# Layer norms of block one: sums taken behind the residual, statistics in two columns, each half normalised in the other half's feed-forward

## The reference

```python
for i in range(2):
    m_lat = jnp.split(cond_lat @ ada_w[i] + ada_b[i], 6, axis=-1)   # m_ctx in the same way
    a_lat = h_lat * (1 + m_lat[1]) + m_lat[0]
    a_ctx = h_ctx * (1 + m_ctx[1]) + m_ctx[0]
    y_ctx, y_lat = mixer(a_ctx, a_lat)             # layer 0: retention, layer 1: neighbourhood
    h_lat = layer_norm(ALPHA * h_lat + m_lat[2] * y_lat, ln_g[i, 0], ln_b[i, 0])
    f_lat = swiglu(h_lat * (1 + m_lat[4]) + m_lat[3], ffn_w13[i], ffn_w2[i])
    h_lat = layer_norm(ALPHA * h_lat + m_lat[5] * f_lat, ln_g[i, 1], ln_b[i, 1])
    # in layer 0 the same three lines for h_ctx
```

## Time and profile before

| | us |
|---|---|
| median of 3 runs (3436.09 to 3440.69) | 3439.42 |
| the profiled execution | 3429.89 |
| its span, first to last instruction | 3428.6 |
| TensorE matmul busy, of the span | 3122.7 (91%) |
| VectorE busy | 2148.2 (63%) |
| ScalarE busy | 1174.0 (34%) |
| GpSimd busy | 194.5 (6%) |
| mean granted TensorE clock | 0.941 |

### The profile page before, as it was taken

How to read it: one execution, slowest core, us unless ns; L and a number is a source line. 1 busy time by engine, 2 the same in 40 slices (tenths; PEclk the granted TensorE clock), 3 DMA queues, 4 the chain that set the end, 5 groups by cost and what they waited for, 6 DMA issues and landing times.

```text
span 3428.6 us, 54650 instructions
## 1 busy us (share of the span) xinstructions
PE 3122.7 (91%) x23382; PEld 2895.1 (84%) x23382; DVE 2148.2 (63%) x3167; ACT 1174.0 (34%) x1455; POOL 194.5 (6%) x223
## 2 busy tenths in 40 slices
PE   6999999699699699979899988999999998899999
PEld 3877878589699676779899988989999998898998
DVE  4676676766566758755565666466656566646665
ACT  2112122233233323234344431244444443124443
POOL 4000000000000002100001001001010100100101
PEclk9989899899899889999999999999999999999999
DMA  7253443488488666545565641235566564123554
GB/s 260 92 181 101 141 156 93 139 246 244 117 236 240 191 209 198 178 123 167 154 173 165 158 120 51 66 108 169 162 187 173 164 159 121 50 67 107 171 160 125
DMA packets 746221, 524.72 MB, mean 153 GB/s; under 512 B 19242, under 2 KB 711660, under 8 KB 745852
## 3 DMA queue, kind: packets, MB, share of 16 engines
q1 hardware_dynamic: 741852, 516.18, 52.1%
q0 software_dynamic: 4128, 5.06, 0.5%
HBM read 520.07 MB, written 2.94 MB: 153 GB/s over the span
## 4 chain that ended last, share of the span: by engine, by line
PE 55%; issue 20%; DVE 13%; ACT 10%; DMA 2%; POOL 0%; SPq 0%; DVEq 0%; ACTq 0%; POOLq 0%
PE bank L453 13%; PE bank L454 12%; PE bank L455 12%; ACT weights_hi L423 7%; DVE side_sums L540 3%; PE bank L561 2%; PE bank L1169 2%; DVE weights_lo L433 1%; ACT mac_gate L1666 1%; DVE mac_prod L1699 1%; PE bank L2034 1%; PE bank L2046 1%; PE bank L2042 1%; PE bank L773 1%; DVE side_sums_odd L540 1%
## 5 line engine op out<-in xcount | busy, mean ns | idle before, releaser
L433 DVE TENSOR_TENSOR weights_lo<-weights_raw,weights_hi 128x2048 fp32r<-128x2048 f32 (+3 forms) x414 | 849.8, 2053 | 413.8 <-ACT weights_hi L423 413.6
L423 ACT ACTIVATE weights_hi<-weights_raw 128x2048 fp32r<-128x2048 f32 (+3 forms) x414 | 709.0, 1713 | 778.5 <-PE bank L455 718.3
L453 PE MATMUL bank<-norm_in_hi,weights_hi 128*128 128x258 f32 x1408 | 406.3, 289 | 21.0 <-DVE mac_prod L1696 11.0
L455 PE MATMUL bank<-norm_in_hi,weights_lo 128*128 128x258 f32 x1408 | 399.1, 283 | 0.0
L454 PE MATMUL bank<-norm_in_lo,weights_hi 128*128 128x258 f32 x1408 | 398.6, 283 | 0.0
L453 PE MATMUL bank<-ffn_in_hi,weights_hi 128*128 128x256 f32 x1056 | 305.4, 289 | 39.0 <-DVE ffn_in_lo L1106 39.0
L454 PE MATMUL bank<-ffn_in_lo,weights_hi 128*128 128x256 f32 x1056 | 304.0, 288 | 0.0
L455 PE MATMUL bank<-ffn_in_hi,weights_lo 128*128 128x256 f32 x1056 | 303.8, 288 | 0.0
L453 PE MATMUL bank<-mix_in_hi,weights_hi 128*128 128x256 f32 x960 | 283.7, 296 | 14.6 <-DVE conv_in L1913 5.8
L453 PEld LDWEIGHTS bank<-norm_in_hi,weights_hi 128*128 128x128 f32 x1408 | 267.7, 190 | 32.9 <-issue 32.7
L454 PE MATMUL bank<-mix_in_lo,weights_hi 128*128 128x256 f32 x960 | 276.9, 288 | 0.0
(11 more groups left out here) (403 smaller groups left out, 6994.8 us busy)
## 6 DMA issues: line engine op xcount, KB each, us to landing
weights_raw<-in_ffn_w SPq DMA_DIRECT2D x132, 512.0 KB, 5.4
weights_raw<-in_w_in SPq DMA_DIRECT2D x120, 512.0 KB, 5.1
side_weights<-in_ada_w SPq DMA_DIRECT2D x86, 576.0 KB, 4.2
weights_raw<-in_ffn_wg SPq DMA_DIRECT2D x88, 512.0 KB, 4.0
weights_raw<-in_ffn_wu SPq DMA_DIRECT2D x88, 512.0 KB, 5.3
weights_raw<-in_ffn_wd SPq DMA_DIRECT2D x64, 704.0 KB, 4.6
weights_raw<-in_ffn_w SPq DMA_DIRECT2D x48, 704.0 KB, 6.1
weights_raw<-in_ret_w_in SPq DMA_DIRECT2D x24, 1024.0 KB, 5.8
```

Source lines behind the costliest of these rows:

```text
L423: k.s.activation(k.w_hi[s % HIGHS][:, 0:n], k.raw[s % RING][:, 0:n], ACT.Copy).then_inc(*k.hi.up())
L433: k.v.tensor_tensor(k.w_lo[s % RING][:, 0:n], k.raw[s % RING][:, 0:n], k.w_hi[s % HIGHS][:, 0:n].bitcast(F32), ALU.subtract).then_inc(*k.l ...
L453: k.te.matmul(out, l[0], r[0], start=first, stop=False)
L455: return k.te.matmul(out, l[1], r[0], start=False, stop=last)
```

## The change

- *Modulation ahead of retention* goes piece by piece, both halves of a piece together, and the first slab of retention waits for each piece (`chunk_by_chunk`) instead of for all.
- *Residual of retention*: ALPHA is applied during the third head (steps 8 and 9), and the gated addition of each piece follows its bank in the last head's slabs 6 to 9. `dve_residual` goes.
- *Sums*: ScalarE squares each piece as soon as it is final; GpSimd adds pieces 0 to 5 and their squares (two additions of 256 columns per piece, 10 per norm, six norms); TensorE takes column sums with 12 one-column matmuls into four banks, tokens on partitions. Statistics are then two columns wide (two halves of 128 tokens). TensorE spreads 1/std and mean/std back over the partitions with four matmuls against the identity.
- *Normalising*: VectorE multiplies and subtracts on pairs of pieces (512 columns, the factor read from a bank); gain, bias, and the modulation are folded into one vector pair per norm (`dve_ln_vectors`), so ScalarE writes high part and full value of each piece, and VectorE the low part. ALPHA is folded into the gain and bias that the next residual uses.
- *Order*: half 1's first norm runs in half 0's tail (sums after up slab 8, spread after slab 10, scaling in steps 11 to 14, high and low parts in the down slabs); half 0's second norm runs in half 1's tail (after up slab 3 and so on); half 1's second norm runs while TensorE multiplies half 0 by the first two value slabs. The first slab that follows a norm waits for it piece by piece.
- *Side finishes* in a tail move from up slabs 7 and 15 to 9 and 17, and the last one from down slab 11 to 15.
- *Neighbourhood mixer*: the input is two tiles, one per half; keys are made in two parts of 256 columns over all pieces, instead of two of 512 columns over half of the pieces.
- *Block two's start*: statistics, scaling, gain and bias, and the input's parts are interleaved by pairs of pieces.

The diff, cut to its core:

```diff
-def act_modulate(k, layer):
-    for half in range(2):
-        for i in range(KD):
+def act_modulate(k):
+    for i in range(KD):
+        for half in range(2):
...
 def pe_retention(k):
-    te.wait_ge(*k.am_lo.at(2 * KD))
...
+            if hd + j == 0:
+                m = chunk_by_chunk(k, [b[:, :] for b in bank], w, k.am, slice(0, 2 * T), KD,
+                                   lambda n: k.am_lo.at(2 * n + 2))
...
 def dve_retention(k):
+                    if hd == RET_H - 1:
+                        n = 2 * (j - 6) + c
+                        v.tensor_tensor(y, y, bank[c][:, :], ALU.add).then_inc(*(k.ev if c else k.dve).up())
...
+                            v.scalar_tensor_tensor(hx, y[:, half * T:(half + 1) * T],
+                                                   k.mods1[:, 0, 2 * KD + n, half:half + 1], hx, ALU.mult,
+                                                   ALU.add).then_inc(*(k.dve if half else k.ln_in).up())
...
+            if hd == RET_H - 2 and j >= 8:
+                hx = flat(k.hb[:, j - 8, :, :])
+                v.tensor_scalar(hx, hx, ALPHA, None, ALU.mult).then_inc(*k.dve.up())
+            if hd == RET_H - 1 and j == 0:
+                for q in range(2):
+                    dve_ln_vectors(k, q)
+                dve_ln_residual_vectors(k, 0)
...
+def pool_ln_sums(k, q, hx):
+    g.wait_ge(k.ln_summed.h, q)
+    for n in range(1, 6):
+        g.wait_ge(k.ln_squared.h, KD * q + n + 1)
...
+        g.tensor_tensor(out=x, in0=hx[:, 0, :] if n == 1 else x, in1=hx[:, n, :], op=ALU.add)
+        g.tensor_tensor(out=xx, in0=squares[0] if n == 1 else xx, in1=squares[n % 2], op=ALU.add).then_inc(*k.ln_added.up())
+
+def pe_ln_sums(k, q, hx):
+    te.wait_ge(k.ln_added.h, 5 * q + 5)
+    te.wait_ge(k.ln_inverted.h, q)
+    for n in range(3):
+        if n:
+            te.wait_ge(k.ln_squared.h, KD * q + 6 + n)
+        x = [(st[:, 0:T], st[:, T:2 * T]), (hx[:, 6, :], sq[:, 0:T]), (hx[:, 7, :], sq[:, T:2 * T])][n]
+        for i in range(4):
+            m = te.matmul(k.AB[i][:, 0:1], x[i // 2][:, (i % 2) * P:(i % 2 + 1) * P], k.ones[:, 0:1], start=n == 0, stop=n == 2)
+
+def dve_ln_scale(k, q, hx, pair):
+    v, x = k.v, hx[:, 2 * pair:2 * pair + 2, :]
+    v.wait_ge(k.ln_spread.h, q + 1)
+    v.tensor_tensor(x, x, bc(k.AB[2][:, 0:T], 2), ALU.mult).then_inc(*k.dve.up())
+    v.wait_ge(*k.dve.now())
+    v.tensor_tensor(x, x, bc(k.AB[3][:, 0:T], 2), ALU.subtract).then_inc(*k.ln_scaled.up())
+
+def act_ln_into(k, q, hx, x, n):
...
+    s.activation(x[0][:, n, :], hx[:, n, :], ACT.Identity, scale=g[:, n:n + 1], bias=b[:, n:n + 1])
+    s.activation(k.sq[:, n, :], hx[:, n, :], ACT.Identity, scale=g[:, n:n + 1], bias=b[:, n:n + 1]).then_inc(*k.af_hi.up())
...
-def pe_ffn(k, x, block):
+def pe_ffn(k, q, block, other):
...
+                              ready=ln_ready(k, q) if i + c == 0 else None)
-        if block is not None and i in (7, 15):
+        if block is not None and i in (9, 17):
...
+        if other is not None and i == LN_AT[other]:
+            pe_ln_sums(k, other, k.hb[:, ln_half(other), :, :])
+        if other is not None and i == LN_AT[other] + 2:
+            pe_ln_spread(k, other)
...
-        if block is not None and i in (3, 11):
+        if block is not None and i in (3, 15):
...
 def dve_ffn_up(k, block, other):
+            if i == at:
+                dve_ln_stats(k, other)
+            if at + 3 <= i < at + 7:
+                dve_ln_scale(k, other, hx, i - at - 3)
...
-def pe_tail(k, hx, block):
-    pe_layer_norm(k, hx, 0)
-    k.te.wait_ge(*k.af_lo.at(KD))
-    pe_ffn(k, k.af, block)
-    pe_layer_norm(k, hx, 1)
+def pe_tail(k, q, block, other):
+    if q != 1:
+        pe_ln_spread(k, q)
+    pe_ffn(k, q, block, other)
...
 def pe_na(k, m):
+    w0, bank0 = pe_slab(k), pe_turn(k)
+    pe_values(k, w0, bank0, 0, (0,), ln_ready(k, 2))
+    pe_ln_sums(k, 3, hx)
+    pe_values(k, w0, bank0, 0, (1,))
+    w1, bank1 = pe_slab(k), pe_turn(k)
+    pe_values(k, w1, bank1, 0, (0,))
+    pe_ln_spread(k, 3)
+    pe_values(k, w1, bank1, 0, (1,))
+    pe_values(k, w0, bank0, 1, (0, 1), ln_ready(k, 3)).then_inc(*k.used.up())
+    pe_values(k, w1, bank1, 1, (0, 1)).then_inc(*k.used.up())
+    pe_side_finish(k, m.block)
```

More of the change, by code:

```diff
@@ L41 @@
 BA_AT = 4
+LN_AT = {1: 8, 2: 3}
 TRI = 3 * P
@@ L1041, in act_ffn_up, with dve_ffn_up @@
         act_hi(k)
-def dve_ffn_up(k, block):
+        if other == 1 and 1 <= i <= 4:
+            for n in (2 * i - 2, 2 * i - 1):
+                act_ln_square(k, 1, k.hb[:, 1, :, :], n, k.before("dve"))
+        if other is not None and i == LN_AT[other]:
+            act_ln_std(k, other)
+def dve_ffn_up(k, block, other):
     v, sided = k.v, block is not None
@@ new lines, in act_tail @@
+def act_tail(k, q, nxt, sided, other, into):
+    s, hx = k.s, k.hb[:, ln_half(q), :, :]
+    if q != 1:
+        act_ln_std(k, q)
+        s.wait_ge(*k.before("pe"))
+        for n in range(KD):
+            act_ln_into(k, q, hx, k.af, n)
+    act_ffn_up(k, sided, other)
+    for i in range(4 * KD // 2):
+        act_hi(k)
+        if other is not None and i % 2 == 0:
+            s.wait_ge(*k.used.at(KF))
+            act_ln_into(k, other, k.hb[:, ln_half(other), :, :], into, i // 2)
+        if i % 4 == 3:
+            act_ln_square(k, nxt, hx, i // 2 - 1, k.ln_in.at(i // 4 + 1))
+            act_ln_square(k, nxt, hx, i // 2, (k.ev.h, ffn_turn(k, KF + i, sided) + 1))
@@ L1109, in dve_tail @@
+def dve_tail(k, q, block, other, into):
+    v, hx, sided = k.v, k.hb[:, ln_half(q), :, :], block is not None
+    _, half, layer, _ = LN_MODS[q]
+    if q != 1:
+        dve_ln_stats(k, q)
+        v.wait_ge(*k.before("pe"))
+        for n in range(KD // 2 + 1):
+            if n < KD // 2:
+                dve_ln_scale(k, q, hx, n)
+            if n:
+                dve_ln_into(k, q, k.af, 2 * n - 2)
+                dve_ln_into(k, q, k.af, 2 * n - 1)
+    dve_ffn_up(k, block, other)
     for i in range(4 * KD // 2):
@@ L1112, in dve_tail @@
             dve_side(k)
+        if other is not None and i % 2 == 1:
+            dve_ln_into(k, other, into, i // 2)
         if i % 4 == 3:
@@ L1398, in act_na @@
 def act_na(k, m):
-    act_modulate(k, 1)
+    act_ln_std(k, 3)
+    k.s.wait_ge(*k.before("pe"))
+    for n in range(KD):
+        act_ln_into(k, 3, k.hb[:, 1, :, :], k.am[1], n)
     for _ in range(4):
@@ L1423, in dve_na @@
     hx = k.hb[:, 0, :, :]
-    v.tensor_scalar(hx, hx, ALPHA, None, ALU.mult).then_inc(*k.dve.up())
+    v.wait_ge(*k.last("dve"))
+    for n in range(KD):
+        dve_ln_residual(k, 2, hx, n)
     t = k.dve.now()
@@ L1448, in block_one @@
     k.decay = m.take("decay_rates", [P, 4 * RET_H])
+    k.ln_vec = m.take("norm_vectors", [P, 16, KD])
     inner = m.at
```

376 lines of the change are left out of this document (217 added, 159 removed).

## The result

The changed kernel takes **3337.52 us** (median of 4 runs, 3334.63 to 3341.03) against 3440.06 for the kernel before in the same comparison: ratio 0.9708, 95% interval 0.9690 to 0.9727, 102.5 us faster. Predicted were 3318, in a range of 3290 to 3350. The profiled execution took 3334.63 us for a span of 3333.3; the span is 95.3 us shorter than before's 3428.6, where the sum had promised 121.2. The profiled execution before is 10.2 us under its median and the one after 2.9 us under its own, so 7 us of the difference between 95.3 and 102.5 lie in which executions were profiled.

What follows compares the result with a forecast made beforehand. TensorE was taken as the bound, idle at layer norms, first slabs and side finishes. The terms sum to 121.2 us gained: 3308.7 us for the profiled execution, 3318 us from the 3439.4 median, range 3290 to 3350.

Steps and rivals of the forecast that it cites:

- Chunked first slab: Start of retention: TensorE starts 8.5 us sooner, but VectorE's side steps then bind; gain 4 us (0 to 8.5).
- Work put into retention: Inside retention: ALPHA scalings and small vector operations delay a late side finish, plus low clock; loss 3.5 us (1 to 6).
- After retention: Norm between retention and tail one: sums, statistics, spread and pipeline reach the feed-forward sooner; gain 16 us (9 to 21).
- Inside the tails: First two tails: moved finishes remove side waits, against added sums, spread, low clock and stalls; gains 10.4 and 8.0 us.
- rival (a): Tails, retention and mixer: cover too narrow, VectorE's additions fall on its 6.24 us chain; gain about 81, 3358 us; chance 0.13.
- Between the halves: Between the first two tails: half 1 already normalised, so the 45.7 us gap and 2.9 low clock go; gain 48.6 us.
- Ahead of the mixer: Neighbourhood mixer's opening: VectorE starts side steps 22 us after the tail, not 34.9; gain 13.5 us, narrower key parts cost 1.1.
- After the mixer: Norm behind the neighbourhood mixer: first half-slab done at 15.9 us, before 32.2, less 1.0 for clock; gain 15.3 us.
- Block two's opening: Ahead of block two: interleaved pairs finish the first slab at about 22 us; gain 10 us (6 to 12.5).
- Rival (b): Tails, retention and elsewhere: low clock after each filled gap does not come; gain 144, 3295 us; chance 0.13.
- (c): At each norm boundary a piece waits for GpSimd's sums, so norms stay on the path; gain 67, 3372 us; chance 0.03.
- (d): Tails: single-column matmuls keep TensorE's clock low, up to 156 us in a tail, making the change slower; chance 0.01.

Runs made afterwards that it cites:

- the second profile: The changed kernel unedited, run again and profiled: ratio 0.9729 to the kernel before, median 3340.8 us; its two tails 219.5 and 213.2 us.
- split statistics: Against the changed kernel, the reciprocal in the tails' norm statistics comes one up slab later, so VectorE needn't wait for the square root; ratio to the kernel before 0.9710.

## Why the prediction was right, and where it was wrong

The range held and the forecast was the likeliest case's: the norms leave TensorE's path, and the largest term is the gap between the halves. The sum was 26 us too high against the profile and 19 against the medians, and the stages are less well known than their decimals say: by the second profile nearly every stage falls short. Where a stage meets its term in one profile alone, that is luck. By its steps:

- **Chunked first slab, +4**: right (3.0 alone in the first head, wait 4.6 to 5.4 as worked out). **Work put into retention, -3.5**: its waits are there as priced (3.35 and 1.53 became 4.50 and 2.52). The profile was 4.4 ahead at the last head where 0.5 was due; that mark lies between 593.9 and 605.6 us in profiles whose edits come later, so single profiles don't settle it.
- **After retention, +16**: 11.4. Statistics, spread and the pipeline took what was foreseen (640.26 to 653.0). The term that failed is the last side sum's delay: 2.9 was charged to VectorE's own work, so a wait of 6.4 was due; it is 9.65, and 6.21 without most of GpSimd's additions. I had put the interference only into a rival. The finish behind the longer wait also took 3.54 us where it took 1.96 before; with the 3.2 of wait that makes 4.8, about the 4.6 that are missing.
- **Inside the tails, +10.4 and +8.0**: 3.9 and 9.3, by the second profile 6.6 and 6.7; so 13.2 and 13.3 in both tails together where 18.4 was forecast (21.3 with tail two's slow start). The closed chain of 6.24 and its one longer step (8.02) are as predicted; three steps of 6.73 beside GpSimd's additions are not. Two terms were too small. "Low clock takes 5.7 per tail": behind the first slab half the mean clock is 0.95 over 211.2 us in tail one and 0.97 over 208.5 in tail two, which at half speed is about 10 and 5 us (8 and 7 by the second profile). Part of it stands behind no wait at all: after the column sums of tail one matmuls of 256 columns start 0.21 apart instead of 0.12 from 707.5 to 710.7. "1.5 of new stalls": TensorE is idle 4.8 us inside tail one and 3.5 inside tail two, mostly in waits for products of 2.38, 2.29 and 2.57, as rival (a) said. The claim that the moved finishes take the side waits away is confirmed (10 us by undoing it).
- **Between the halves, +48.6**: 42.7. I had let the whole 45.7 and the low-clock start go; 2.99 us of wait remain (3.58 in the second profile, over the 3 that the prediction allowed) and the second tail still starts at the low level (27 matmuls in 5 us).
- **Ahead of the mixer, +13.5 less 1.1**: 8.9 at the first side finish, 16.5 at the mixer's end. VectorE as the bound was right, its first side step came 28.4 us after the tail instead of 22 (1104.10 less 1075.69): the spread is late because TensorE reaches it behind 72 matmuls, sums and a mean clock of 0.74 (window 1077.77 to 1094.04). The 7.6 us gained later in the mixer are the clock of that one profile: the second gains 8.8 at the first finish and 8.8 at the end. That the row of 12.4 is met and passed is luck; by the second profile it is 3.6 short.
- **After the mixer, +15.3**: 13.6 at the 24th matmul, then tail three lost 2.2, with no idle time in either trace and a mean clock from that matmul on of 0.99, before 1.00. **Block two's opening, +10**: 7.9.
- **Block two itself, nothing**: -12.3, half of the shortfall. That unchanged work keeps its time was an assumption nowhere written down; the profile before had a mean clock of 0.94 and so room to move either way.

Rival (a) was right in its mechanism at two places: 3.4 us behind retention, and waits for products of 4.7 in tail one, not 40 in all. Of its signs two came, a wait for products behind slab 17 and a tail over 215 (tail one, 218.6 and 216.0 us from its first matmul to its last, of which 4.5 are its slow first slab half, priced elsewhere in the sum). By the rule of the Trainium skill, "SBUF — State Buffer", section "Who interferes with whom", a VectorE instruction with two SBUF inputs and a GpSimd instruction that reads SBUF shut each other out for the whole instruction; the trace agrees in kind: weights' low part 2.82 instead of 2.29 us, and GpSimd's addition between 0.72 and 2.61. Where the rest of the 43 us of full exclusion went, no run shows. Rival (b) did not come, (c) and (d) neither.

## What to carry to other kernels

A wait taken from TensorE is worth its length only if its granted clock stays: split statistics removed 2.4 us of wait and shortened one product step by 1.8, and the two tails took 434.4 us instead of 432.1 and 432.7. Take a second profile of the same kernel before explaining a stage: here an untouched stage differed by 7 us between two. When a side task must be finished for a consumer, ask which step the consumer waits for and move what stands in front of that one; shifting steps behind it does nothing. Price helpers on GpSimd by what VectorE runs beside them, and put them where VectorE waits.

## What was not expected of the hardware

- In the tails a single-column group of 18 matmuls takes 2.06 us behind running work (862.19) and 3.97 behind a wait of 4.5 us or more (983.08 with the finishes back): a late side finish is paid twice. Behind waits of 1.4 to 3.4 us it took 2.1 to 2.4.
- GpSimd's additions cut from 256 columns to one still took up to 2.1 us: those of a piece to the sum 0.19 to 2.12 (median 1.32), those of the squares 0.18 to 1.38 (median 0.19).
- One pair of additions per slab costs VectorE's chain 0.49 us, and two pairs in one slab cost the same 0.49.
- The time at the low clock differs by steps: block two's mixers lie near 464, 467, 470.5 and 473 us with the same instructions and the same idle time, and the later part of the neighbourhood mixer is 201 or 208 us, nothing between.
